# One layer of a hybrid decoder trunk: every fourth low half of the output projection made by an accumulating DMA

## The reference

```
h    = rmsnorm(x) ;  mh = rmsnorm(mem)
proj = h @ w_in                      # q, k, v, gate of three branches, and 3 x 2048 gate logits
ua   = (dilated_mixture(qa, ka, va) * silu(za)) @ w_proj_a     # 12 heads of 128
ub   = (forgetting_attention(qb, kb, vb, log_f) * silu(zb)) @ w_proj_b    # 8 heads of 128
um   = (memory_attention(qm, *split(mh @ w_mem_kv)) * silu(zm)) @ w_proj_m   # 4 heads of 256
g    = sigmoid(gate logits + b_gate)
merged = g0 * ua + g1 * ub + g2 * um
out  = x + merged @ w_out            # w_out is 2048 x 2048
```

## Time and profile before

| | |
|---|---|
| median of the runs | 1215.74 us |
| the profiled execution | 1215.12 us, its span 1213.3 us |
| TensorE matmuls busy | 1205.5 us, 99% of the span |
| VectorE busy | 681.2 us, 56% |
| ScalarE busy | 535.4 us, 44% |
| GpSimd busy | 35.1 us, 3% |
| DMA | 235.4 MB, 194 GB/s on average |
| output projection | about 1121 to 1210 us of the span |

### The profile page before, as it was taken

How to read it: one execution, slowest core, us unless ns; L and a number is a source line. 1 busy time by engine, 2 the same in 40 slices (tenths; PEclk the granted TensorE clock), 3 DMA queues, 4 the chain that set the end, 5 groups by cost and what they waited for, 6 DMA issues and landing times.

```text
span 1213.3 us, 14994 instructions
## 1 busy us (share of the span) xinstructions
PE 1205.5 (99%) x5596; PEld 1003.1 (83%) x5596; DVE 681.2 (56%) x871; ACT 535.4 (44%) x672; POOL 35.1 (3%) x22
## 2 busy tenths in 40 slices
PE   8999999999999999999999999999999999999998
PEld 7888888888888888888888888888888888888887
DVE  6656554555556565565565555565556555555643
ACT  5654444434534534444444453434435443443432
POOL 0000000010000000000000000000000000000000
PEclk9999999999999999999999999999999999999999
DMA  9667555555565564564564564467557546755761
GB/s 329 209 198 270 195 194 175 196 171 177 174 200 173 173 209 163 173 206 166 183 203 161 187 205 160 165 205 236 182 176 229 202 156 225 212 194 196 272 211 49
DMA packets 121459, 235.40 MB, mean 194 GB/s; under 512 B 7575, under 2 KB 11852, under 8 KB 120908
## 3 DMA queue, kind: packets, MB, share of 16 engines
q1 hardware_dynamic: 108592, 218.44, 54.1%
q10 hardware_dynamic: 12828, 16.42, 4.6%
HBM read 231.16 MB, written 6.06 MB: 196 GB/s over the span
## 4 chain that ended last, share of the span: by engine, by line
PE 98%; DMA 1%; DVE 0%; ACT 0%; SPq 0%; issue 0%; DVEq 0%
PE acc L970 30%; PE acc L972 30%; PE acc L971 30%; PE side L993 2%; DMA w_raw<-in_x_dram 1%; PE side L1010 1%; PE side L1034 1%; PE side L1006 1%; PE side L1024 1%; DMA w_raw<-in_w_in_dram 1%; PE side L1044 0%; PE side L1042 0%; PE side L1040 0%; PE side L1011 0%; PE side L1099 0%; PE side L1069 0%
## 5 line engine op out<-in xcount | busy, mean ns | idle before, releaser
L610 DVE TENSOR_TENSOR w_lo<-w_raw,w_hi 128x1024 fp32r<-128x1024 f32 x408 | 498.5, 1225 | 482.9 <-ACT w_hi L340 482.8
L340 ACT ACTIVATE w_hi<-w_raw 128x1024 fp32r<-128x1024 f32 x408 | 431.0, 1061 | 603.2 <-PE acc L972 590.6
L970 PE MATMUL acc<-w_hi,hT_hi 128*128 128x512 f32 x1152 | 454.1, 394 | 0.9 <-DVE hT_lo L632 0.6
L972 PE MATMUL acc<-w_hi,hT_lo 128*128 128x512 f32 x1152 | 449.0, 390 | 0.0
L971 PE MATMUL acc<-w_lo,hT_hi 128*128 128x512 f32 x1152 | 448.3, 389 | 0.0
L970 PEld LDWEIGHTS acc<-w_hi,hT_hi 128*128 128x128 f32 x1152 | 216.4, 188 | 45.3 <-DVE w_lo L610 0.7
L972 PEld LDWEIGHTS acc<-w_hi,hT_lo 128*128 128x128 f32 x1152 | 216.2, 188 | 45.5
L971 PEld LDWEIGHTS acc<-w_lo,hT_hi 128*128 128x128 f32 x1152 | 216.5, 188 | 43.3
L970 PE MATMUL acc<-w_hi,mT_hi 128*128 128x512 f32 x256 | 101.1, 395 | 0.0
L972 PE MATMUL acc<-w_hi,mT_lo 128*128 128x512 f32 x256 | 99.8, 390 | 0.0
L971 PE MATMUL acc<-w_lo,mT_hi 128*128 128x512 f32 x256 | 99.7, 389 | 0.0
(11 more groups left out here) (138 smaller groups left out, 549.8 us busy)
## 6 DMA issues: line engine op xcount, KB each, us to landing
w_raw<-in_w_in_dram SPq DMA_DIRECT2D x143, 1024.0 KB, 5.0
w_raw<-in_w_mem_kv_dram SPq DMA_DIRECT2D x16, 1024.0 KB, 6.1
w_raw<-in_w_out_dram SPq DMA_DIRECT2D x16, 1024.0 KB, 5.1
w_raw<-in_w_proj_a_dram SPq DMA_DIRECT2D x12, 1024.0 KB, 5.0
w_raw<-in_w_proj_m_dram SPq DMA_DIRECT2D x8, 1024.0 KB, 5.0
w_raw<-in_w_proj_b_dram SPq DMA_DIRECT2D x8, 1024.0 KB, 5.1
group<-bias_tiles ACTq DMA_DIRECT2D x5, 768.0 KB, 4.2
group<-in_b_gate_dram ACTq DMA_DIRECT2D x12, 256.0 KB, 5.9
```

The lines of the kernel that those rows point to most:

```text
L340: act.activation(whi[:, s % RING], raw[:, slot, UK * (s % 2):UK * (s % 2) + UK], ACT.Copy)\
L610: dve.tensor_tensor(wlo[:, s % RING], raw[:, (s // 2) % RING, UK * (s % 2):UK * (s % 2) + UK], whi[:, s % RING].bitcast(F32), ALU.subtract ...
L970: pe.matmul(banks[t][:], hi, whi[:, s % RING, j], start=first and j == 0, stop=False)
L972: return pe.matmul(banks[t][:], lo, whi[:, s % RING, j], start=False, stop=last and j == UK - 1)
```

## The change

In the output projection every unit with s % 4 = 2 (s = 2, 6, ..., 30, eight of 32) gets its low half in another way. ScalarE makes `w_hi` as before, waits for its own `hi_done`, and then writes the negated high half into the slot of `w_lo`. GpSimd waits for that (`neg_done`) and issues a DMA that reads the unit's 0.5 MB of `w_out` from HBM a second time and adds it onto `w_lo` in SBUF. VectorE, instead of the subtraction, waits for `hi_done` and sets one column of a spare tile, which keeps the count of `lo_done`. TensorE waits for the DMA's semaphore `lo_added` before such a unit, beside its wait for `lo_done`. GpSimd's loop stands behind its last root.

```diff
+ADDED = 2
...
+    neg_done, lo_added = sem("neg_done"), sem("lo_added")
...
+            for i in range(NCH * CU // RING):
+                s = RING * i + ADDED
+                n, k = s // CU, UK * (s % CU)
+                pool.wait_ge(neg_done, i + 1)
+                pool.dma_start(wlo[:, s % RING], w_o[:, k:k + UK, n * CW:(n + 1) * CW], accum_op=ALU.add)\
+                    .then_inc(lo_added, 16)
...
             for s in range(NCH * CU):
                 hi(u0, s, lc, MERGE_U)
+                if s % RING == ADDED:
+                    act.wait_ge(hi_done, u0 + s + 1)
+                    act.activation(wlo[:, s % RING], whi[:, s % RING].bitcast(F32), ACT.Copy, scale=-1.0)\
+                       .then_inc(neg_done, 1)
                 if s in (4, 5):
                     merged_split(NCH - 1, s - 4)
...
             for s in range(NCH * CU):
-                lo(u0, s)
+                if s % RING == ADDED:
+                    dve.wait_ge(hi_done, u0 + s + 1)
+                    dve.memset(spare[:, 0:1], 0.0).then_inc(lo_done, 1)
+                else:
+                    lo(u0, s)
...
+                if s % RING == ADDED:
+                    pe.wait_ge(lo_added, 16 * (s // RING + 1))
                 if s < NCH * CU - 1:
```

## The result

The changed kernel takes 1240.87 us (two runs, 1240.70 and 1241.03) against 1215.74: a ratio of 1.0207, 95% interval 1.0163 to 1.0251, so 25.1 us more, about at the 2% line and not clearly on either side of it. The forecast was 1234 us and its range 1221 to 1262.

A forecast was written before the change was run, and what follows sets the result against it. The prediction took TensorE, busy 99% of the span, as the bound. Stalls of 6.1 (unit 2), 6.8 (unit 6) and 5.4 us (six later units), together 18.3, on 1215.1 gave 1233.4, or 1234 on the median's scale; range 1221 to 1262.

The forecast's parts named there:

- two long stalls, six short ones: TensorE's expected waits before touched units: 5 to 8 us at units 2 and 6, about 1 us at six later ones.
- The rooms: Time from negation's end until TensorE would stand still: 2.1 us at unit 2, 1.4 at unit 6, 5.5 at later units.
- the likeliest case: Stalls of 5 to 8 us at two units, up to 1.7 at six; 1228 to 1240 us, chance 0.36.
- within 2%: Whole kernel slower, but by less than 24.3 us; chance of staying inside 2% given as 0.59.
- The sum: Stalls on TensorE added up: 6.1 us at unit 2, 6.8 at unit 6, 5.4 over six later units; 18.3 us.
- L in the quiet part: Time from negation's end to the accumulate's completed semaphore with quiet DMA engines: 5.1 + 1.3 = 6.4 us.
- GpSimd's part: GpSimd's building of the accumulate's descriptors, taken as 1.3 us, between its cheapest and dearest operations.
- Unit 2: First touched unit, DMA engines busy: 8.2 us from negation to landing, less 2.1, a stall of 6.1 us.
- Unit 6: Second touched unit, DMA engines busy: 8.2 us from negation to landing, less 1.4, a stall of 6.8 us.
- The clock: Rival: TensorE's clock falls in the stalls at units 2 and 6, up to 5.4 us more, 1239 us; chance 0.10.
- the short accumulate: Rival: the accumulate takes at most 5.5 us in the gaps, only units 2 and 6 stall; 1217 to 1228, chance 0.17.
- The long one: Rival: slow accumulate, every touched unit pays, over 2% slower from 7.2 us per accumulate; up to 1260 us, chance 0.35.

The follow-up runs named there:

- early_two: The changed kernel with only units 2 and 6 accumulated, the six later ones subtracted again; 1234.09 us, ratio 1.0152.
- ahead_two: The changed kernel with units 6 to 30 negated two units early, alternate buffers, residual loads behind unit 6's negation; 1216.29 us, ratio 1.0001.
- late_residual: The changed kernel with the four residual loads (2 MB) behind unit 8's high half instead of ahead of unit 0; 1244.91 us, one run.
- late_six: The changed kernel with units 2 and 6 subtracted again and only units 10, 14, ..., 30 accumulated; 1222.34 us, ratio 1.0053.
- clock: The changed kernel with 60 and 40 dummy transposes ahead of TensorE's waits of units 2 and 6; 1236.55 us, ratio 1.0174.
- late_wait: The changed kernel with TensorE's DMA wait moved behind a touched unit's eight matmuls that read only `w_hi`; 1230.05 us, ratio 1.0113.
- units_3: The changed kernel with units 3, 7, ..., 31 touched instead of 2, 6, ..., 30; 1248.6 us, one run.

## Why the prediction was right, and where it was off

The kind was right in each step: two long stalls, six short ones, no stall before a unit that still subtracts, VectorE's relief worth nothing, and ScalarE's and SyncE's added work hidden (early_two and ahead_two). The rooms were right to 0.1 us. The time, 1240.87, is in the range, but just past the likeliest case (1228 to 1240), and whether it is within 2%, as forecast, the interval leaves open. The sum was 18.3 us where 25.3 were lost, because of these terms:

- *L in the quiet part*, 6.4 us: measured 6.5 (unit 10), and up to 6.8 (unit 30), with stalls of 1.01 to 1.31 us for five of the six units where 0.9 stood. The transfer was right for a reason: the landing less GpSimd's part is 6.3 - 1.2 = 5.1 us, the row of the 1 MB weight load, with the destination counted as bytes. GpSimd's part, 1.3 us forecast and 1.2 measured, was luck: it was picked between 0.70 and 2.57 us of other operations. The 0.3 to 0.4 us before GpSimd starts were in no term.
- *Unit 2*, 8.2 us as the middle between 6.4 and 10.1: measured 10.2, the upper end, so 8.2 us of stall and not 6.1. late_residual gives 2.2 us of it to the residual loads. The bound was in the earlier trace rows, and those very loads were still in flight when GpSimd issued; the middle was the wrong choice there.
- *Unit 6*, the same 8.2: measured 6.8, so 5.4 us and not 6.8. The forecast compared with where the weight loads lay before. But unit 2's stall had moved unit 6 by 8 us and the loads by another amount, and they mostly missed each other: 0.30 of the 0.52 MB moved between 1151.5 and 1153 us with hardly a weight load beside them.
- *The clock* was a rival with a chance of 0.10 and stood outside the sum. It came true: 4.4 us, within its bound of 5.4. The row for it was there, 0.70 after more than 2 us without a matmul, and the forecast's two long stalls were longer than that. A mechanism whose condition the forecast itself fulfils belongs in the sum. With the 4.4 that it was, the sum would have been 1238. The Trainium skill ("TensorE: Matmul & The Clock Gate", § Part 1) has an idle TensorE fall to half its clock; the 0.50 from 1136 to 1140 us agrees.
- *Unit 26's 2.7 us* were not forecast at all (last section).

Against the rival rows: the short accumulate is refuted by late_six (6.5 us where it gives none). The long one set its mark at L = 7.2 us in the quiet part and is refuted too, by 6.5 to 6.8 us in five of six units. The 2% line was reached by unit 2 and the clock, not by it. The Trainium skill's two figures ("DMA: Bandwidth & Descriptors", § Anatomy of one DMA, and "Collectives: The Full Stack", § The bandwidth ceiling) made 3.2 us for the plain DMA and 4.4 for the reducing one. The runs have 4.4 and 6.3, both above, and still 3.7 and 5.1 without GpSimd's own 0.7 and 1.2 us. The half rate that the second names fits the rates in the next section.

## What to carry to other kernels

Price a transfer that replaces arithmetic by its latency against the room it has at each place, not by its bandwidth: eight equal DMAs cost 8, 5, 1 and (ahead_two) 0 us, by where they stood. The start of the stage was the worst place here, since the producing engine was late there and other loads were in flight. Where a forecast has TensorE stand still for 5 us or more, the matmuls behind the stall belong in the sum at the lower clock level (here 1.5 and 2.9 us). Shorter stalls can cost this too (next section).

## What the runs showed of the hardware

The changed kernel's DMA rate by fortieths of 1209 to 1222 us, with GpSimd's accumulate alone on the engines in the first burst and an output store in the second, and one queue's line in that stretch (packets, MB, share). Below it is the accumulate's queue from 1215.5 to 1216.4 and from 1216.4 to 1217 us:

```profile
DMA  0000000035999999761200699960000000000000
GB/s 0 0 0 0 0 0 0 0 57 101 151 183 195 202 202 208 132 120 32 69 0 0 227 378 353 378 246 32 13 0 0 0 0 0 0 0 0 0 0 0
...
q8 instruction: 1, 0.02, 0.5%
...
q0 software_dynamic: 1, 0.00, 0.2%
...
q0 software_dynamic: 3, 0.00, 6.9%
```

- An accumulate runs at some 200 GB/s where the store reaches 378, at full engine shares: half the rate. Over the whole execution the eight took 1.6 times the engines' time of plain ones (2.1% to 1.3%).
- The single long stall of unit 26, 1.6 us over its neighbours, falls together with that one fetch of instructions by the DMA engines. Its packet is 16 KB and holds one engine for 0.96 us from 1215.48 on. In that time nearly nothing of the accumulate moves, and its last packets start at 1216.43, as the fetch ends. late_six (2.51 us) and late_residual (2.30) have the same order of packets at unit 26. In the trace of clock, where a fetch falls into unit 2's accumulate, its L is 0.9 us longer. That the fetch is the cause is read from the order of packets and was not tested. It is not the only way to such a length: unit 22's in late_wait took as long with no fetch, beside 1.1 MB of weight loads.
- In the changed kernel the clock fell while the engine waited, and came back only after thirteen matmuls of work behind the first stall and seven behind the second.
- The length of a stall alone did not decide. In units_3 the matmuls between 1186 and 1189 us, behind unit 15's stall of 2.99 us, ran at the lower level, 0.43 us apart (row below). In late_residual some eight did so a little behind a stall of 2.30 us (unit 26). Behind the 2.71 us of unit 26 in the changed kernel none did.
- Transposes that ended 2.3 us before the wait did (clock) did not hold the clock up at unit 2; those that ended 1.1 us before did at unit 6.

```profile
1186.00:1189.00 3.00, 3.00 (x9) 2.33 (x8) 0.00 (x0) 0.00 (x0) 0.00 (x0) 0.50 0.42 162
```
